# Gating the attention heads inside their PSUM bank, in a three-layer transformer kernel

## The reference, cut to what matters

```
ya = merge(diff_attention(...)) * silu(ga)      # diff: rms-normed per head, with a gain sub_g
yb = merge(stick_breaking_attention(...)) * silu(gs)
yc = merge(forgetting_attention(...)) * silu(gf)
y  = concatenate([ya, yb, yc], axis=-1) @ w_out
return x + rms_norm(y, g_post)
```

## Time and profile before

| what | value |
|---|---|
| runs | 2145.85, 2170.09, 2173.84 us |
| median | 2170.09 us |
| profiled execution, span | 2171.3 us |
| mean granted TensorE clock of it | 0.960 |
| PE busy | 2062.2 us, 95% |
| DVE busy | 743.2 us, 34% |
| ACT busy | 867.9 us, 40% |
| POOL busy | 659.7 us, 30% |

### The profile page before, as it was taken

The page is one execution under the profiler, slowest core; times in us unless marked ns, Lnnn a source line. Parts: engine busy times, 40 slices in busy tenths (PEclk is TensorE's granted clock), DMA queues, the critical chain, the costliest instruction groups (busy, mean ns, idle before and its releaser), DMA issues.

```text
span 2171.3 us, 25579 instructions
## 1 busy us (share of the span) xinstructions
PE 2062.2 (95%) x9552; PEld 1617.0 (74%) x9552; DVE 743.2 (34%) x1278; ACT 867.9 (40%) x1706; POOL 659.7 (30%) x278
## 2 busy tenths in 40 slices
PE   8999999899899999889998998999999999999998
PEld 6866766776777677667767777888878878888886
DVE  3154355324433526551324268111044141111002
ACT  4354455424433535553314355233344343323222
POOL 2422321220232232123202434443310433444442
PEclk9999999999899999899957999999999999999999
DMA  4211211110121121112103222222210232222222
GB/s 141 87 47 61 78 49 40 59 68 20 59 78 59 50 77 59 49 40 78 50 0 117 79 77 79 97 90 92 90 50 4 96 135 78 97 97 97 97 97 88
DMA packets 43755, 157.50 MB, mean 73 GB/s; under 512 B 6144, under 2 KB 6400, under 8 KB 43264
## 3 DMA queue, kind: packets, MB, share of 16 engines
q1 hardware_dynamic: 42640, 148.65, 20.0%
q10 hardware_dynamic: 1008, 7.34, 0.9%
HBM read 151.78 MB, written 4.19 MB: 72 GB/s over the span
## 4 chain that ended last, share of the span: by engine, by line
PE 78%; DVE 13%; ACT 5%; issue 4%; DMA 0%; POOL 0%; DVEq 0%; ACTq 0%; POOLq 0%; SPq 0%
PE bank L574 10%; PE bank L575 10%; PE bank L576 10%; PE bank L577 10%; PE bank L579 10%; PE bank L578 10%; PE bank L664 6%; PE bank L708 5%; DVE probs L1216 3%; PE bank L689 2%; ACT probs L917 1%; DVE probs L1252 1%; PE bank L668 1%; PE bank L673 1%; PE bank L627 1%
## 5 line engine op out<-in xcount | busy, mean ns | idle before, releaser
L557 POOL TENSOR_TENSOR w_hl<-w_raw,w_hl 128x1024 fp32r<-128x1024 f32 x274 | 659.5, 2411 | 1487.3 <-ACT w_hl L783 1486.8
L783 ACT ACTIVATE w_hl<-w_raw 128x1024 fp32r<-128x1024 f32 x274 | 286.9, 1057 | 399.4 <-DMA w_raw<-wstream 398.9
L574 PE MATMUL bank<-act_hl,w_hl 128*128 128x512 f32 x1056 | 433.2, 410 | 2.1 <-DVE act_hl L1106 2.1
L576 PE MATMUL bank<-act_hl,w_hl 128*128 128x512 f32 x1056 | 418.1, 396 | 0.0
L575 PE MATMUL bank<-act_hl,w_hl 128*128 128x512 f32 x1056 | 418.1, 396 | 0.0
L577 PE MATMUL bank<-w_hl,act_hl 128*128 128x512 f32 x672 | 264.8, 394 | 3.4 <-POOL w_hl L557 2.3
L578 PE MATMUL bank<-w_hl,act_hl 128*128 128x512 f32 x672 | 262.9, 391 | 0.0
L579 PE MATMUL bank<-w_hl,act_hl 128*128 128x512 f32 x672 | 262.8, 391 | 0.0
L574 PEld LDWEIGHTS bank<-act_hl,w_hl 128*128 128x128 f32 x1056 | 203.9, 193 | 44.4 <-DVE act_hl L1106 2.6
L576 PEld LDWEIGHTS bank<-act_hl,w_hl 128*128 128x128 f32 x1056 | 202.3, 192 | 44.8
L575 PEld LDWEIGHTS bank<-act_hl,w_hl 128*128 128x128 f32 x1056 | 203.5, 193 | 41.4 <-issue 1.9
(11 more groups left out here) (205 smaller groups left out, 2519.8 us busy)
## 6 DMA issues: line engine op xcount, KB each, us to landing
w_raw<-wstream SPq DMA_DIRECT2D x274, 512.0 KB, 3.4
x_res<-x SPq DMA_DIRECT2D x4, 512.0 KB, 5.6
g_post<-post_gains ACTq DMA_DIRECT2D x4, 512.0 KB, 3.7
x_spill<-x_res ACTq DMA_DIRECT2D x1, 2048.0 KB, 7.2
x_res<-x_spill ACTq DMA_DIRECT2D x1, 2048.0 KB, 8.6
out<-x_res SPq DMA_DIRECT2D x4, 512.0 KB, 2.6
probs<-w_gates ACTq DMA_DIRECT2D x1, 1024.0 KB, 9.3
mask_b<-masks SPq DMA_DIRECT2D x1, 288.0 KB
```

Source lines behind the costliest of these rows:

```text
L557: nc.gpsimd.tensor_tensor(w_hl[:, slot, 1].rearrange("p c n -> p (c n)"), w_raw[:, slot, :], w_hl[:, slot, 0].rearrange("p c n -> p (c n)" ...
L574: pe.matmul(out_ap, wh, ah, start=start, stop=False)
L576: return pe.matmul(out_ap, wl, ah, start=False, stop=stop)
L783: nc.scalar.activation(w_hl[:, b % RING, 0].rearrange("p c n -> p (c n)"), w_raw[:, b % RING, :], ACT.Copy).then_inc(s_high_done, 1)
```

## The change

Product, high part and low part stay, with the same sizes. The product now writes into the bank that it reads, y_tmp isn't used for it any more, high and low part read the bank, and the bank is freed by the low part. A new semaphore, gated, tells ACT that the product is there. The semaphore y_low goes: who waited for it now waits for the release of the bank. DVE no longer waits for its own last low part. The dilated kind's instructions are the same.

```diff
                 take(("Y", l, kind, p), BT)
+                if kind != "dil":
+                    mark("gated", (l, kind, p))
                 mark("y_high", (l, kind, p))
-                mark("y_low", (l, kind, p))
...
                     if g["tag"] == "o":
-                        pe.wait_ge(s_y_low, MARKS["y_low", (g["l"], g["kind"], last - 1)])
+                        pe.wait_ge(*drained(("Y", g["l"], g["kind"], last - 1)))
...
                 if tag == "g" and gi > 4:
-                    act.wait_ge(s_y_low, MARKS["y_low", prev_kind(g["l"], g["kind"]) + (3,)])
+                    act.wait_ge(*drained(("Y",) + prev_kind(g["l"], g["kind"]) + (3,)))
...
                 else:
-                    act.wait_ge(*drained(("Y", l, kind, p)))
-                    src = y_tmp[:, :]
+                    act.wait_ge(s_gated, MARKS["gated", (l, kind, p)])
+                    src = bank_of(("Y", l, kind, p))[:, :]
...
                 scalar = sub_g[:, l:l + 1] if kind == "diff" else 1.0
-                nc.vector.scalar_tensor_tensor(out=y_tmp[:, :], in0=ps[:, :], scalar=scalar, in1=gate[:, p, :],
-                                               op0=ALU.mult, op1=ALU.mult).then_inc(freed(("Y", l, kind, p)), 1)
+                nc.vector.scalar_tensor_tensor(out=ps[:, :], in0=ps[:, :], scalar=scalar, in1=gate[:, p, :],
+                                               op0=ALU.mult, op1=ALU.mult).then_inc(s_gated, 1)
                 dve.wait_ge(s_y_high, MARKS["y_high", (l, kind, p)])
-                dve.wait_ge(*drained(("Y", l, kind, p)))
-                nc.vector.tensor_tensor(y_hl[:, p, 1, :], y_tmp[:, :], y_hl[:, p, 0, :].bitcast(f32), ALU.subtract)\
-                    .then_inc(s_y_low, 1)
-                dve.wait_ge(s_y_low, MARKS["y_low", (l, kind, p)])
+                nc.vector.tensor_tensor(y_hl[:, p, 1, :], ps[:, :], y_hl[:, p, 0, :].bitcast(f32), ALU.subtract)\
+                    .then_inc(freed(("Y", l, kind, p)), 1)
```

More of the change, by code:

```diff
@@ L345, in build @@
     s_y_high = nc.alloc_semaphore("y_high")
-    s_y_low = nc.alloc_semaphore("y_low")
+    s_gated = nc.alloc_semaphore("gated")
     x_in = [nc.alloc_semaphore(f"x_in{t}") for t in range(TT)]
```

## The result

| | before | after |
|---|---|---|
| median of 20 runs | 2170.85 us | 2169.93 us |
| lowest and highest | 2138.92, 2204.38 | 2163.05, 2197.99 |
| profiled execution, span | 2171.3 | 2163.9 |
| its mean granted clock | 0.960 | 0.969 |

The ratio is 1.0116, with a 95% interval of 1.0084 to 1.0148: slower by 1.2%, and within the 2% that count as no change. This ratio compares only the runs within 1.5% of each kernel's own fastest, so it doesn't agree with the two medians.

A forecast was written before the change was run, and what follows sets the result against it. TensorE, busy 95%, was taken as the bound. Median 2170.1 plus 12.9 us of bank waits plus 1.7 us for one short clock fall gave 2184.7, said as 2185 us; range 2156 to 2212, own range 2180 to 2194.

The forecast's parts named there:

- Price of one release, 1.35 us, and its twelve places: Bank 6 freed by low part, not product: PE waits up to 1.35 us more at steps 8 and 17-18, 12.9 us.
- Step 13: Heads turned at step 13 of 19, six times: no added wait; tightest cover 0.2 us, in fox of layer 0.
- Operands in the bank: High part reading the bank takes 597 ns against 631; low part 692 against 693.
- the write: DVE's product written into a bank: taken as no cost, bound 0.06 us each, 0.7 us on 12 products.
- All on PE, nothing absorbed: The added 12.9 us of waits for bank 6 all fall on PE, busy 95%, and lengthen the run.
- The rival of hidden waits: PE later waits for DVE or ACT anyway, so the lost time vanishes: 2171 us; chance 0.05.
- The short stretches of half clock: New PE waits buy short clock falls, at most 1.7 us each: one counted, bounds none and six (0 and 10 us).
- The long stretches: Long half-clock stretch in fox, 25.0 us between layers: the median run has one before and after; chance 0.46.
- the rival for that case: Median run has no long clock fall in fox: 2159 us, though PE waits 12.9 us more; chance 0.27.
- step 8 of fox: PE waits 0.78 us ahead of pair 0's turn, 0.33 us more behind it; may buy further clock falls.
- The size of a long stretch: Fox from pair 0's turn to first output product: 37.67 us against 62.70; three runs differ by about 24 us.
- Two long stretches in one run: Rival: fox falls to half clock in both layers, 2210 us; no run of three showed it; chance 0.17.

The follow-up runs named there:

- the shifted pair: Seven matmuls put behind pair 3's turn in sb: on the kernel before, lowest group 2145.9 us; on the changed kernel, median 2172.2 us.
- The filled wait: Changed kernel with nine unused matmuls ahead of pair 3's turn (not dil), where PE stood idle: median 2159.3 us.
- The late release of pair 0: Kernel before, y_tmp kept, with bank 6 freed by the low part instead of the product for pair 0 alone: lowest group 2160.6 us.
- the three with y_tmp and late release: Kernel before with bank 6 freed by the low part, for all pairs, pair 2 or pair 0: lowest runs 2175.9, 2161.4 and 2158.7 us.
- own bank: Changed kernel with pair 3 turned into bank 4 instead of bank 6: lowest group 2147.6 us.
- step 16: Changed kernel with pair 2's heads turned one step sooner, HEADS_AT = (8, 13, 16, 18): median 2151.9 us.
- the second trace: Trace of the kernel before with bank 6 freed by the low part for all pairs; its six runs took 2175.9 to 2215.9 us.

## Why the prediction came out as it did

- **Price of one release, 1.35 us, and its twelve places: right.** 1.37 at pair 3 and 0.41 us from pair 0 to pair 1 in fox (21.99 us for 21.58); 12.4 us of waits in all for 12.9. Step 13 stayed without a wait.
- **Operands in the bank: right.** High part 34 ns shorter, low part the same; the write, which no row had shown, 7 to 8 ns, well inside the 60 allowed.
- **All on PE, nothing absorbed: right,** by the account above and by all waits of PE together, 13.0 us more in the shifted pair. The rival of hidden waits fell.
- **The short stretches of half clock: the term that was mis-sized.** I counted one, 1.7 us, with bounds of 0 and 10. Measured: 23 us more at half clock, 11.6 us lost, above even the upper bound of six falls. The bound was wrong in kind: a fall right behind the long wait at pair 3 came only about every second time (15 of 29), which is some 5 us, and as much again was lost in slow stretches that stand elsewhere. The filled wait shows that idle gaps are the cause of it (10 us back at the same length), and not how they reach that far.
- **The long stretches: the step that failed.** I took the median run to have one in both kernels, as the forecast said, so 2185. After the change only 4 of 20 runs had one, so the median is a run without: 2169.9. By the rival for that case, to which I had given 0.27, it should have been 2159; its 11 us too little are mostly the short stretches, for which it had none. I had said that more waiting at step 8 of fox might make them likelier. The late release of pair 0 puts nearly that wait there and changes nothing in the count (6 of 12), so this step was wrong. The place where they start was read rightly: with PE's wait ahead of pair 0's turn filled, none of 36 runs had one.
- **The size of a long stretch,** 24 to 25 us, was read off two fox stages; between the groups it is 26 to 31 us. The dense products behind fox start slow as well (4.7 us at half clock, some 2.4 us lost); and 24 was read off three runs, of which the fast one (2145.85) lies 4 us above the median of its group. Two long stretches in one run, which I called unseen, were by time and clock in 4 of the first 20 runs of the kernel before.
- That the time lies in the range (2156 to 2212) and within 2% is in good part luck. It lies outside of the forecast's own range (2180 to 2194), and the range held because these errors had opposite signs: 10 us too few for short stretches, some 28 too many for the long one (2184.7 + 10 - 28 = 2167, of 2169.9 measured).

**Open:** why the changed kernel has the long stretches in 4 of 20 runs, while the kernel before has them in 56 of 104 and the three with y_tmp and late release in 14 of 24. The release is not the reason. With the product in the bank and no work put ahead of a wait it is 7 of 49 (changed, own bank, step 16, shifted), so the bank operands may be, or only the timing ahead of fox; moving fox by 1.6 us did not settle it, and none in five runs of the kernel before with pair 3 in bank 4 speaks for the timing. So that the two medians are equal is not explained to the end: the 27 us on one side are, what stands against them is only counted. Open is also where the second half of the clock's share comes from.

## What to carry to other kernels

Keep a buffer that frees a contended bank early: saving an SBUF tile by working in the bank moved its release by two operations and put 12 us of waits on the engine that bounds the kernel. Where TensorE is the bound, don't price a wait at its length alone: here 13.0 us less of it gave 21.8, 4.8 gave 9.5, and 12.4, 8.7 and 4.7 us more cost 27, 22 and 18. Look at the granted clock of the whole run beside it, over several runs. A bank that is idle at that moment, or work in the gap, costs less. Before a difference of one percent is believed, look whether the runs fall into groups; two medians can agree by accident.

## What the hardware showed that I had not expected

- A TensorE wait of 0.78 us, in a stage of scores with 64 rows, values with 64 columns and transposes, can be followed by 65 us at 1.2 GHz, until dense products have run for 3 to 5 us (1084.13 to 1148.99; 524.90 to 589.70 in the second trace). PE was not idle in that time: 62.87 of 64.86 us are busy. With three matmuls of 0.23 us each in the gap, none of the 36 runs of three kernels had it; of the kernel before 56 of 104 had.
- A wait of 2.15 to 2.29 us ahead of four transposes was followed within 1.3 us of its end by 3.4 us at 1.2 GHz in 15 of 29 cases, one of 0.78 to 0.85 us in none of 23, and the gap of 2.2 us filled with nine matmuls in none of 6.
- The same kernel took 2138.9 to 2204.4 us, 3%, in three groups; their mean clocks give 67 and 64 us more at half clock from group to group, one long stretch each.
- The same work of 200 us had 3.4 us at half clock in three executions, 13.7 and 17.1 in two others.
- The product written to the bank that it reads took 8 ns more than the one written to SBUF, 700 against 692 ns.
